# A hybrid decoder layer in fp32: the input's two tiles loaded in halves from two queues, and one small transpose moved between them

## The reference, cut to what matters

```python
h = rmsnorm(x, g_mix)                       # x (1, 256, 1024), g_mix (1024,)
proj = h @ w_in                             # w_in (1024, 4608)
q, k, v, u, gate_a, gate_c = split(proj)    # 3 x 512, 1024, 2 x 1024
o = moba_attention(q, k, v)                 # 8 heads of 64; one block of 256, so causal attention
cz = conformer_conv(u + b_glu)              # GLU, 31-tap depthwise conv, layernorm, silu
merged = sigmoid(gate_a) * (o @ w_attn_up) + sigmoid(gate_c) * (cz @ w_conv_pw + b_conv_pw)
x = x + merged @ w_out
h = rmsnorm(x, g_ffn)
x = x + square(relu(h @ w_ff1)) @ w_ff2     # 1024 -> 4096 -> 1024
return rmsnorm(x, g_final)
```

## Time and profile before

| | us |
|---|---|
| median of 3 runs (354.77 to 354.86) | 354.84 |
| the profiled execution's own time | 354.16 |
| its span | 352.4 |
| TensorE busy in the span | 346.3 |
| VectorE busy | 251.0 |
| ScalarE busy | 192.1 |

### The profile page before, as it was taken

One profiled execution on the slowest core, in us unless ns is written; L12 is line 12 of the kernel. 1 busy time (PEld: TensorE's weight loads), 2 busy tenths in 40 slices (PEclk: granted clock), 3 DMA queues, 4 the chain that ended last, 5 costly groups with the idle time before them and its releaser, 6 DMA issues.

```text
span 352.4 us, 4590 instructions
## 1 busy us (share of the span) xinstructions
PE 346.3 (98%) x1729; PEld 287.2 (82%) x1729; DVE 251.0 (71%) x308; ACT 192.1 (55%) x237; POOL 3.5 (1%) x13
## 2 busy tenths in 40 slices
PE   8999999999999999999999999999999999999994
PEld 5888888787778888888888888888888888888884
DVE  2969999999989889956756836639366394563813
ACT  4995654688886458434764535525355163551534
POOL 1000000000000000000000000000000000000000
PEclk9999999999999999999999999999999999999998
DMA  8999455434543365692636471944728537260003
GB/s 275 350 387 376 163 190 189 168 121 149 187 144 119 121 238 173 246 262 100 229 126 240 160 251 67 306 170 144 246 86 304 172 126 247 104 238 0 0 0 120
DMA packets 34430, 64.24 MB, mean 182 GB/s; under 512 B 1360, under 2 KB 6000, under 8 KB 34416
## 3 DMA queue, kind: packets, MB, share of 16 engines
q1 hardware_dynamic: 34112, 63.57, 53.2%
q10 hardware_dynamic: 304, 0.48, 0.4%
HBM read 63.00 MB, written 1.05 MB: 182 GB/s over the span
## 4 chain that ended last, share of the span: by engine, by line
PE 98%; DVE 0%; issue 0%; DVEq 0%; ACT 0%
PE ps L943 21%; PE ps L945 20%; PE ps L944 20%; PE ps L1179 17%; PE ps L1181 9%; PE ps L930 4%; PE ps L989 2%; PE ps L1000 1%; PE ps L1043 1%; PE ps L1068 1%; PE ps L970 1%; PE ps L1141 0%; PE ps L1226 0%; PE ps L1225 0%; PE ps L1224 0%; PE ps L984 0%
## 5 line engine op out<-in xcount | busy, mean ns | idle before, releaser
L943 PE MATMUL ps<-w_hi,a_lo 128*128 128x512 f32 x272 | 107.5, 395 | 0.0
L945 PE MATMUL ps<-w_lo,a_hi 128*128 128x512 f32 x272 | 106.1, 390 | 0.0
L944 PE MATMUL ps<-w_hi,a_hi 128*128 128x512 f32 x272 | 106.0, 390 | 0.0
L1179 PE MATMUL ps<-b_both,w_hi 128*128 128x512 f32 x256 | 90.8, 399 | 0.0
L1181 PE MATMUL ps<-b_both,w_lo 128*128 128x256 f32 x256 | 71.9, 281 | 0.0
L871 DVE TENSOR_TENSOR w_lo<-raw,w_hi 128x2048 fp32r<-128x2048 f32 x28 | 63.5, 2288 | 6.4 <-ACT w_hi L606 6.4
L396 ACT CAST w_hi<-raw 128x2048 fp32r<-128x2048 f32 (+1 forms) x30 | 53.6, 1794 | 16.8 <-PE ps L945 16.7
L657 DVE TENSOR_TENSOR w_lo<-raw,w_hi 128x2048 fp32r<-128x2048 f32 x26 | 59.3, 2285 | 3.4 <-ACT w_hi L396 3.3
L943 PEld LDWEIGHTS ps<-w_hi,a_lo 128*128 128x128 f32 x272 | 51.1, 188 | 11.1 <-issue 0.7
L945 PEld LDWEIGHTS ps<-w_lo,a_hi 128*128 128x128 f32 x272 | 51.0, 188 | 11.0
L944 PEld LDWEIGHTS ps<-w_hi,a_hi 128*128 128x128 f32 x272 | 51.1, 188 | 10.0
(11 more groups left out here) (130 smaller groups left out, 258.0 us busy)
## 6 DMA issues: line engine op xcount, KB each, us to landing
raw<-in_w_ff_dram SPq DMA_DIRECT2D x32, 1024.0 KB, 5.5
raw<-in_w_in_dram SPq DMA_DIRECT2D x14, 1024.0 KB, 5.5
raw<-in_w_out_dram SPq DMA_DIRECT2D x4, 1024.0 KB, 5.0
raw<-in_w_in_dram SPq DMA_DIRECT2D x14, 256.0 KB, 5.3
raw<-in_w_attn_up_dram SPq DMA_DIRECT2D x2, 1024.0 KB, 5.0
raw<-in_w_conv_pw_dram SPq DMA_DIRECT2D x2, 1024.0 KB, 5.1
res<-in_x_dram SPq DMA_DIRECT2D x2, 512.0 KB, 3.7
raw<-in_w_in_dram SPq DMA_DIRECT2D x4, 128.0 KB, 4.1
```

The source lines that it names most:

```text
L943: nc.tensor.matmul(dst, lo[:, tok], w_hi[:, slot, k], start=start, stop=False, skip_group_check=seeded)
L944: nc.tensor.matmul(dst, hi[:, tok], w_hi[:, slot, k], start=False, stop=False, skip_group_check=seeded)
L945: return nc.tensor.matmul(dst, hi[:, tok], w_lo[:, slot, k], start=False, stop=stop, skip_group_check=seeded)
L1179: nc.tensor.matmul(ps[:, TB + c], w_hi[:, slot, k, cols], b_both[:, kk].rearrange("p a t -> p (a t)"), start=kk == 0, stop=False)
```

## The change

Each tile of `x` is loaded in two transfers of 64 rows. SyncE issues rows 0 to 63 of tiles 0 and 1 where it issued whole tiles; ScalarE issues rows 64 to 127 of tile 0, then `g_mix`, then rows 64 to 127 of tile 1. Both halves count on the same semaphore, so the waits go from 16 to 32. On TensorE the wait for `g_mix` and the transpose of `gmix_rows` are moved from before tile 0 to between tile 0 and tile 1.

```diff
+X_ROWS = P // 2
...
             for t in range(TT):
-                sp.dma_start(res[:, t], x_v[:, t]).then_inc(x_full[t], 16)
+                sp.dma_start(res[0:X_ROWS, t], x_v[0:X_ROWS, t]).then_inc(x_full[t], 16)
...
         def _(act):
+            act.dma_start(res[X_ROWS:P, 0], x_v[X_ROWS:P, 0]).then_inc(x_full[0], 16)
             act.dma_start(gmix_rows, g_mix.rearrange("l (c p) -> (l c) p", p=P)).then_inc(gmix_full, 16)
+            act.dma_start(res[X_ROWS:P, 1], x_v[X_ROWS:P, 1]).then_inc(x_full[1], 16)
...
-            act.wait_ge(x_full[0], 16)
+            act.wait_ge(x_full[0], 32)
             square_input(0)
             high(2)
-            act.wait_ge(x_full[1], 16)
+            act.wait_ge(x_full[1], 32)
             square_input(1)
...
             pe.wait_ge(ident_made, 1)
-            pe.wait_ge(gmix_full, 16)
-            transpose(ps[:, SB0, 0:KD], gmix_rows).then_inc(gmix_tr, 1)
             for t in range(TT):
-                pe.wait_ge(x_full[t], 16)
+                pe.wait_ge(x_full[t], 32)
                 for k in range(KD):
                     last = transpose(x_chunk(k)[:, t * P:t * P + P], res[:, t, k * P:k * P + P])
                     if t == TT - 1 and k % 2 == 1:
                         last.then_inc(x_tr, 1)
+                if t == 0:
+                    pe.wait_ge(gmix_full, 16)
+                    transpose(ps[:, SB0, 0:KD], gmix_rows).then_inc(gmix_tr, 1)
```

## The result

The changed kernel takes 357.39 us (median of 6 runs, 357.09 to 358.18) against 354.82 us for the kernel before in the same comparison: a ratio of 1.0086, 95% interval 1.0076 to 1.0097, which is 2.7 to 3.4 us (the two medians themselves lie 2.6 apart). The prediction was 355.0, no change, with a range of 354.5 to 355.5. The profiled execution has a span of 355.8 us, 3.4 more than that of before.

The account below looks back on a forecast made before the run. TensorE, busy 98% of the span, was taken as the bound. Earlier start worth 0.16 us, `gmix` +0.30: +0.14 on 354.16 gives 354.30; the runs' median lies 0.68 higher, so 354.98, say 355.0 us, range 354.5 to 355.5.

Parts of the forecast that it names:

- What bounds the kernel: Whole kernel: TensorE, busy 98% of the span, is the bound; its first transposes do not wait for `x`.
- Landing of tile 0: Loads at the head: tile 0's halves land at 4.15 us, bounds 4.05 and 4.5, against 4.05 before.
- its twin for tile 1: Loads at the head: tile 1, landed at 5.39 us before, was given no delay in the sum.
- rival 2: Half tiles land late at half rate: tile 0 at 5.3, +0.73 us; tile 1 at 7.9, +2.0; chance 0.09.
- The clock: Head of TensorE: idle time before 5.70 us could keep it at 1.2 GHz longer, on top of rival 2; no size.
- The issues: Load issues at the head: SyncE's halves 0.26 to 0.42 us each, 0.4 taken; ScalarE's two more 0.26 to 0.59, free.
- The order of the transposes: TensorE's head: tile 0 starts at 4.25, 0.24 earlier, worth 0.16 us; moved `gmix_rows` transpose costs 0.30; sum +0.14.
- The 0.3 for the small transpose behind tile 0: TensorE between the tiles: the moved transpose of `gmix_rows` takes 0.3 us, bounds 0.11 and 0.39.
- Rival 1: TensorE's wait at 4.29 was for the vector's load, its transpose nearly free later: -0.1 to -0.3 us, 354.6; chance 0.10.
- Rival 3: TensorE's clock rises at another time: earlier saves at most 0.6 us (354.3), 1 us later costs about 0.5 (355.5); chance 0.06.

## Why the prediction was wrong

**What bounds the kernel** was read rightly: `x` was not waited for, and nothing could be gained by an earlier landing. The forecast failed on what could be lost.

**The step that failed is "Landing of tile 0"**, and its twin for tile 1: 4.15 was taken, with 4.5 as the upper bound of the ordinary case, and tile 1 was given no delay. Tile 0 landed at some 5.6, and tile 1 at 7.95 instead of 5.39. The step reasoned that both halves carry together the bytes of one transfer, and rival 2 was marked down because both are in flight together and so together fill all partitions. The queue rows show that they are not: one half moves, then the other, at some 220 GB/s instead of 410. One queue alone gives the same landings (5.58 and 7.87), so the second queue is not the cause; rows 32 to 95 at the full rate, and the columns at 313, show that the partitions are. The prediction described this mechanism in rival 2, with landings of 5.3 and 7.9, priced it at +0.7 to +2.0 plus the clock, and gave it 0.09. It quoted the rule that decides it and then set it aside with an argument that no row of the trace bore out; "no row shows a half tile" was a reason for a larger chance, not for a smaller one.

**The clock.** "An idle TensorE before 5.70 could keep the clock at 1.2 GHz longer on top" was the right worry, unpriced. In the profiled execution of the changed kernel the clock had risen when tile 0 came and fell in the second wait; in that of the halves on one queue it had not risen by then. The price is 1.50 by the chain, 1.44 when TensorE was kept busy.

**The issues** were taken at 0.26 to 0.42 and 0.4. They took 0.50 to 0.58, one of them 0.84. The bound came from a small vector (0.26) and from 128 rows (0.42); 64 rows took more than either. The first weights were issued 0.6 late; in three other runs (kept busy, small transpose in front, halves exchanged) they were 0.35 late and the issue of `g_mix` took 1.12 to 1.13.

**The order of the transposes** was right: start at 4.23 (4.25), sum +0.14, measured +0.2 with zero in the interval. The 0.3 for the small transpose behind tile 0 is borne out where the clock was already high: in the run with whole tiles on two queues the last transpose of tile 0 starts at 5.37 and ends, at that pace, at 5.48, and the small one runs from 5.57 to 5.79, 0.31 for it. (Tile 1 starts at 5.80, but it also landed at about 5.8 there.) Rival 1 is out: in the kernel before the vector's packets had moved by 2.15, long before the gap at 4.29, and in the run with the order alone the 0.33 of idle time came at 6.12, 5.4 us after its load was issued.

**Rival 3** is seen in the kernel before and its kin: the steps fall to 0.11 at 5.7 in the profile before, at 6.5 in the run with the order alone, and by 4.4 in the run with fewer dummies. It may be part of why runs of one kernel spread over a microsecond (353.88 to 355.21 for the 26 of before in one comparison; only one was profiled), but it is not the difference: no run of the changed kernel is under 357.09.

What stays open: why an issue of 64 rows takes 0.58 where 128 rows take 0.38 and 32 rows 0.42; why the first half to move has short packets and still lands no earlier; what decides which queue goes first; and why, with two queues, the column halves land late in the profiled run, and perhaps in the other slow run of the nine.

## What to carry to other kernels

Leave a load of 128 partitions whole, or split it by columns (here still +0.9 us), not by halves of the partitions: those moved at half the rate here, and a second queue did not bring in the other half at the same time. When a load with slack is touched, price what its lateness triggers: here 2.0 us of landing brought 1.5 us of half clock, and a tiny vector queued behind a half tile landed 5.3 us after its issue. A rule like that of the Trainium skill (SBUF — State Buffer, Door 1), which spoke against this change and which no row of the trace contradicted, deserves more than one chance in ten.

## What the runs showed of the hardware that was not expected

- The time of an issue went with the shape of the transfer: 0.35 to 0.43 us for 128 rows (whole tiles or half their columns), 0.50 to 0.64 for 64 rows, 0.42 for 32 rows (0.58 right behind one of 64); one right behind a 64-row issue, on either queue, took up to 0.84 (the next half tile on SyncE) and 1.13 (`g_mix` on ScalarE).
- Transfers issued within 0.01 us of each other on two queues did not share the 16 DMA engines: from 1.5 to 3.0 the one queue moved 0.18 MB and the other nothing. Which one went first changed between kernels with the same loads.
- The first 256 KB that fill only half of the partitions go out in packets of 158 ns, as fast as a whole tile's, but land at 4.35 (halves on one queue), later than the 512 KB of a whole tile (4.05).
- In the changed kernel TensorE's clock was up at 5.71 right behind 1.38 us of idle time, and in the run with one halved tile it stayed up over 1.24 us of it; in the changed kernel it had fallen after 1.38 and another 1.07.
